# Two mixer projections from plain fp32 matmuls to three fp32r passes, with the remainders on VectorE in layer 0 and on GpSimd in layer 1

## The chip, the core and the metric

One core of a Trainium2 chip runs the whole program once. The metric is the device time of one execution in microseconds (us); the lower the better. The five engines of the core (TensorE, VectorE, ScalarE, GpSimd and SyncE, which issues the transfers) have queues of their own and meet at semaphores. The profile calls them PE, DVE, ACT, POOL and SP; PEld is TensorE's loading of stationary operands, which overlaps its matmuls.

## What is computed

A block of 256 tokens with 1024 features passes two layers of the first network (feed-forward, token mixer, feed-forward, a layer norm after each) and then two layers of a second one. All data is fp32. The part that the change touches is the first product of each token mixer:

```python
def token_mixer(h, w_in, pool_w, pool_scale, rel_bias, lb, norm_g, w_branch, w_out):
    proj = h @ w_in          # [256, 1024] @ [1024, 6920]
    (a, q, k, v, qi, ki, wi, hq, hf, hi, hg, gates) = jnp.split(proj, MIX_SPLITS, axis=-1)
    y_a = pool_mixer(a, pool_w, pool_scale)
    y_b = sparse_attention(q, k, v, qi, ki, wi, rel_bias)
    y_c = hgrn2(hq, hf, hi, hg, lb, norm_g)
    g = jax.nn.sigmoid(gates)
    return (g[0] * (y_a @ w_branch[:256]) + g[1] * (y_b @ w_branch[256:512])
            + g[2] * (y_c @ w_branch[512:])) @ w_out
...
    h = modulate(layer_norm(x), mod, 1)
```

## The kernel before

**Panels.** Every weight matrix is cut into panels of 256 output columns, 1 MB each, and streamed in the order of use through four SBUF slots by SP (`load`, L529). A panel's load waits until TensorE has finished the panel four places earlier. A product of the kernel is a `Gemm` in `plan()`; `Gemm(f"mix{l}", 15)` are the first 3848 columns of `w_in` in 15 panels, `gate{l}` the gates in 12.

**Two ways to multiply.** A plain panel (`features`, L674) multiplies the fp32 weights with the fp32 activations H; the profile shows each such matmul as two MATMUL rows of 256 columns, 32 a panel. A split panel (`split_up`, L703 to L705 for a stage's first panel, and `split_half`, L687 to L689 for the rest) has the fp32r rounding of the weights (high) and of the activations, and both remainders (low), and sums three products, high x high, high x low and low x high: 48 MATMUL rows of 256 columns. ScalarE makes a half panel's high part by a copy (`high`, L1379), another engine then its low part by a subtraction in place (`low`): VectorE for all the feed-forward products of the first network (L86), GpSimd for `even` and `up0` in the second (L1340). High parts lie in a ring of two panels, so ScalarE writes one only when TensorE has used the panel two places before (`wait_used`). TensorE waits for each half's `low_made`.

**The mixer's first stage.** Panels 0 to 4 and 9 to 14 hold features on the partitions, 6 to 8 are computed with tokens on the partitions (`tokens`, L765), and 5 is a mixed one: half a panel of features (L1232) and 16 narrow matmuls (L1235). ScalarE takes each result out of PSUM (`evac`, L76). All four accumulators of `acc` are in use in turn.

**Riders.** While TensorE works on these panels, VectorE computes something else: the modulation vectors, from 1 MB panels of their own ("cond units": `cond_weigh`, L1959; 15 of them in each mixer). A cond unit is a multiply with row sums of [128, 1024] by a row of conditions that is spread over the partitions: two such instructions in layer 0, four in layer 1 (there two condition rows are served). The units alternate between two SBUF slots, and SP loads unit i only when `cond_done` says that unit i - 2 is finished. SP runs one list in order: panel u, unit u, panel u + 1, unit u + 1, and so on. So a panel's load also stands behind the wait of the unit before it:

```python
load(g, it * 4 + u, u)         # after TensorE has finished panel u - 4
load_cond(g.name, it, u)       # waits cond_done of unit u - 2
```

**Around it.** `layer_norm` runs before each stage on four engines; for j = 0 (the one ahead of a mixer) it writes H alone, the even chunks by ScalarE and the odd ones by VectorE, and TensorE starts chunk by chunk. For j = 1 and 2 (ahead of split panels) it also makes high and low parts of the activations (L1414, L1416, and L86 for the subtraction). After the 15 panels `stage_end` joins TensorE, VectorE and ScalarE: none goes on until all three have come. Then come `pool`, `attention` and `hgrn`, with the gate panels between.

## Time and profile before

| | us |
|---|---|
| median of 3 runs | 3105.27 (3104.22 to 3106.03) |
| profiled execution, its time | 3109.24 |
| its span | 3107.4 |
| TensorE busy | 2791.2 (90%) |
| VectorE busy | 1874.8 (60%) |
| ScalarE busy | 1034.5 (33%) |
| GpSimd busy | 197.8 (6%) |
| last mean matmul of the layer norm ahead of mixer 0, of mixer 1 | 256.98, 986.97 |
| stage of mixer 0, first matmul to the join | 267.25 to 373.26 |
| stage of mixer 1, first matmul to the join | 997.29 to 1103.30 |

The two stages are 106.0 us each, 7% of the span together. Busy shares are averages over stages of different kinds; what a stage gains by the change has to be read in that stage.

### The profile page before, as it was taken

Reading aid. Unit: us, or ns where it says so; the run is one execution under the profiler, and the core shown is the slowest. Engines: PE = TensorE matmul, PEld = TensorE weight load, DVE = VectorE, ACT = ScalarE, POOL = GpSimd, SP = SyncE. Lnnn points to the kernel's source line nnn. Section 1 sums busy time; section 2 is a strip of 40 time slices with the busy share of each in tenths; the row PEclk is TensorE's granted clock in tenths of the full one; section 3 lists DMA queues with packets and bytes.
Section 4 is the critical chain, followed back from the end, with each engine's and each line's share of the span. In section 5 each row is a group of like instructions: output and inputs, shape, how many; then the busy total and the mean of one; then the engine's idle time right before and its main releaser. Section 6 shows DMA issues by size and latency. Waiting matters only on the chain.

```text
span 3107.4 us, 47661 instructions
## 1 busy us (share of the span) xinstructions
PE 2791.2 (90%) x18018; PEld 2348.9 (76%) x18018; DVE 1874.8 (60%) x3213; ACT 1034.5 (33%) x1334; POOL 197.8 (6%) x89
## 2 busy tenths in 40 slices
PE   2999999999999998999799467999999799969998
PEld 2998877999998887899688344587745567648887
DVE  5785254677785844657482675577733576662881
ACT  1432132443542123243433542333301544441211
POOL 0000000000000000000044000144300000000000
PEclk9999999999999998999899579999999999979999
DMA  7786633577673932456151101122252211103441
GB/s 267 269 320 253 231 109 141 203 263 281 222 274 129 342 123 84 175 188 240 66 211 55 63 1 63 67 95 94 83 219 111 82 68 68 55 14 122 150 173 70
DMA packets 109673, 469.59 MB, mean 151 GB/s; under 512 B 7020, under 2 KB 60856, under 8 KB 62136
## 3 DMA queue, kind: packets, MB, share of 16 engines
q1 hardware_dynamic: 109496, 467.19, 41.6%
q8 instruction: 116, 1.90, 0.2%
q14 instruction: 61, 0.50, 0.0%
HBM read 466.10 MB, written 1.06 MB: 150 GB/s over the span
## 4 chain that ended last, share of the span: by engine, by line
issue 52%; PE 30%; DVE 8%; DVEq 6%; ACT 3%; ACTq 1%; POOLq 0%; PEldq 0%; PEld 0%
PE accs L786 9%; DVEq L2570 3%; PE accs L674 3%; DVE arena L2547 2%; PE accs L687 2%; PE accs L689 2%; PE accs L688 2%; PE accs L1134 2%; PE accs L1135 2%; PE accs L1136 2%; DVE normed L86 1%; ACT arena L76 1%; PE mix L1182 1%; DVE arena L86 1%; PE mix L833 1%
## 5 line engine op out<-in xcount | busy, mean ns | idle before, releaser
L687 PE MATMUL accs<-normed_r,arena_r 128*128 128x256 f32 (+2 forms) x1864 | 585.6, 314 | 20.4 <-DVE cond_panel_r L86 6.1
L688 PE MATMUL accs<-arena_r 128*128 128x256 f32 (+1 forms) x2090 | 594.8, 285 | 0.0
L689 PE MATMUL accs<-normed_r,panel_r 128*128 128x256 f32 (+2 forms) x1872 | 585.0, 312 | 0.0
L674 PE MATMUL accs<-normed,panel 128*128 128x256 f32 x2176 | 483.8, 383 | 6.7 <-ACTq L469 3.0
L674 PEld LDWEIGHTS accs<-normed,panel 128*128 128x128 f32 x2176 | 413.9, 192 | 71.3 <-issue 4.6
L86 DVE TENSOR_TENSOR panel_r<-panel,arena_r 128x1024 fp32r<-128x1024 f32 (+1 forms) x240 | 319.7, 1332 | 130.5 <-ACTq L1380 91.2
L688 PEld LDWEIGHTS accs<-arena_r 128*128 128x128 f32 x2090 | 395.5, 189 | 2.2 <-issue 0.2
L687 PEld LDWEIGHTS accs<-normed_r,arena_r 128*128 128x128 f32 (+1 forms) x1864 | 351.2, 188 | 56.4 <-issue 13.0
L1379 ACT ACTIVATE arena_r<-panel 128x1024 fp32r<-128x1024 f32 (+1 forms) x240 | 275.3, 1147 | 303.4 <-PE accs L689 114.6
L689 PEld LDWEIGHTS accs<-normed_r,panel_r 128*128 128x128 f32 (+1 forms) x1872 | 350.8, 187 | 23.9
L2547 DVE SCALAR_TENSOR_TENSOR arena<-accs,vectors,arena 128x189 f32<-128x189 f32 (+2 forms) x704 | 279.3, 428 | 95.2 <-issue 66.0
L1340 POOL TENSOR_TENSOR panel_r<-panel,arena_r 128x1024 fp32r<-128x1024 f32 x74 | 183.6, 2481 | 2046.6 <-ACTq L1387 2045.0
L786 PE MATMUL accs<-arena,panel 128*128 128x256 f32 (+1 forms) x960 | 284.8, 458 | 0.6 <-DVEq L2568 0.6
L786 PEld LDWEIGHTS accs<-arena,panel 128*128 128x128 f32 x960 | 183.1, 191 | 100.8 <-issue 84.7
L76 ACT ACTIVATE arena<-accs 128x512 f32<-128x512 f32 (+2 forms) x128 | 75.3, 588 | 458.4 <-PE accs L674 198.6
L91 DVE SCALAR_TENSOR_TENSOR residual<-accs,mods,residual 128x256 f32<-128x256 f32 x96 | 46.4, 484 | 291.9 <-PE accs L786 177.4
L687 PE MATMUL accs<-arena_r 128*128 128x256 f32 x704 | 202.5, 288 | 6.4 <-DVEq L2000 6.4
L689 PE MATMUL accs<-arena_r,panel_r 128*128 128x256 f32 x704 | 200.1, 284 | 0.0
L76 ACT ACTIVATE arena<-residual 128x512 f32<-128x512 f32 (+1 forms) x64 | 36.9, 577 | 370.4 <-DVEq L2599 300.4
L1386 ACT ACTIVATE arena_r<-panel 128x1024 fp32r<-128x1024 f32 x74 | 78.5, 1061 | 229.8 <-PE accs L689 200.9
L76 ACT ACTIVATE arena<-arena 128x512 f32<-128x512 f32 (+7 forms) x107 | 97.3, 909 | 161.3 <-DVEq L2493 54.6
L687 PEld LDWEIGHTS accs<-arena_r 128*128 128x128 f32 x704 | 135.3, 192 | 7.5 <-issue 6.9
(373 smaller groups left out, 4151.8 us busy)
## 6 DMA issues: line engine op xcount, KB each, us to landing
panel<-w SPq DMA_DIRECT2D x250, 1024.0 KB, 4.9
panel<-w SPq DMA_DIRECT2D x48, 1408.0 KB, 7.8
cond_panel<-wc SPq DMA_DIRECT2D x56, 1024.0 KB, 7.0
normed<-wc SPq DMA_DIRECT2D x48, 1024.0 KB, 7.5
arena<-wc SPq DMA_DIRECT2D x16, 1024.0 KB, 5.7
residual<-xs SPq DMA_DIRECT2D x2, 1024.0 KB, 8.3
residual<-crows SPq DMA_DIRECT2D x2, 512.0 KB, 8.8
arena<-cond_row_kept SPq DMA_DIRECT2D x2, 512.0 KB, 6.8
```

The costliest lines, as they stand in the source:

```text
L76: i = self.eng.activation(*a, **k)
L86: i = self.eng.tensor_tensor(*a, **k)
L674: mm = pe.matmul(acc[b][:, o:o + ntok], w[:, k * PANEL + j * P:k * PANEL + j * P + P], rhs(k), start=(k == 0), stop=(k == KD - 1))
L687: pe.matmul(out, hi[:, k, 0:m], src_hi(k), start=clear and k == 0, stop=False, skip_group_check=True)
L688: pe.matmul(out, hi[:, k, 0:m], src_lo(k), start=False, stop=False, skip_group_check=True)
L689: mm = pe.matmul(out, lo[:, k, 0:m], src_hi(k), start=False, stop=last and k == n - 1, skip_group_check=True)
L786: mm = pe.matmul(acc[a % BANKS][:, o:o + ntok], w[:, k * PANEL + j * P:k * PANEL + j * P + P], src(part * kper + k), start=first, stop=(pa ...
L1340: pool.tensor_tensor(lo, half_panel(g, u, j), hi, ALU.subtract)
L1379: act.eng.activation(split_parts(g, u, j)[0], half_panel(g, u, j), ACT.Copy)
L1386: act.eng.activation(split_parts(g, u, j)[0], half_panel(g, u, j), ACT.Copy)
L2547: dve.eng.scalar_tensor_tensor(out=out, in0=src, scalar=scale, in1=out, op0=ALU.mult, op1=ALU.add)
L2570: dve.drain()
```

## The change

Both `mix` products become split ones. In each mixer TensorE now does 48 MATMUL rows of 256 columns in the place of 32 for the feature panels and for the three token panels (`mix_tokens`), and for panel 5 24 in the place of 16, with the 32 narrow rows as they were (`mix_keys`). ScalarE makes the high parts (`mix_high`, a ring of two panels in the room of the gates), two halves a panel and one for panel 5: 29 copies a mixer. The 29 subtractions are VectorE's in mixer 0 (`mix_low`, ahead of each cond unit) and GpSimd's in mixer 1 (`POOL_LOW`). The layer norm ahead of a mixer now makes high and low parts of the activations as well; the fp32 values stay in H for the gates and for panel 5. Loads, cond units, gates and all that follows stay as they were.

```diff
@@ plan
-                  Gemm(f"mix{l}", 15), Gemm(f"gate{l}", 12), ...
+                  Gemm(f"mix{l}", 15, split=True, kept=True), Gemm(f"gate{l}", 12), ...
+POOL_LOW = ('mix1',)
+        mix_hi = [region(7472 + i * KD * PANEL, KD, PANEL, of=arena_r) for i in range(2)]
+        m_hi, m_lo = region(15664, KD, T, of=arena_r), region(17712, KD, T, of=arena_r)
+        def mix_halves(u):
+            return ((0, 2),) if u == 5 else ((0, 1), (1, 1))
+        def norm_target(l, j):
+            if j == 2:
+                return G[f"in{l + 1}0"] if l + 1 < DEPTH else None
+            if j == 1:
+                return G[f"in{l}1"]
+            return G[f"mix{l}"] if G[f"mix{l}"].split else None
@@ tensor
+            def mix_keys(g, u):
+                b = acc_open(g, 0, u)
+                w = slots[(g.p0 + u) % SLOTS]
+                split_half(g, 0, u, 0, acc[b][:, 0:T], lambda k: m_hi[:, k, :], lambda k: m_lo[:, k, :], True, True, first_used)
+                for tb in range(2):
+                    for k in range(KD):
+                        mm = pe.matmul(acc[b][:, T + 8 * tb:T + 8 * tb + 8], H[:, k, T + tb * P:T + tb * P + P],
+                                       w[:, k * PANEL + P:k * PANEL + P + 8], start=False, stop=(k == KD - 1), skip_group_check=True)
+                mm.then_inc(ready[b], 1)
+            def mix_tokens(g, u):
+                hi, lo = mix_hi[u % 2], slots_r[(g.p0 + u) % SLOTS]
+                b = acc_open(g, 0, u)
+                pe.wait_ge(S("low_made"), split_count(g, 0, u, 1))
+                for tb in range(2):
+                    t = slice(tb * P, tb * P + P)
+                    for k in range(KD):
+                        pe.matmul(acc[b][:, tb * T:tb * T + T], m_hi[:, k, t], hi[:, k, :], ...)
+                        mm = pe.matmul(acc[b][:, tb * T:tb * T + T], m_lo[:, k, t], hi[:, k, :], ...)
+                mm.then_inc(first_used, 1)
+                for tb in range(2):
+                    for k in range(KD):
+                        mm = pe.matmul(acc[b][:, tb * T:tb * T + T], m_hi[:, k, tb * P:tb * P + P], lo[:, k * PANEL:k * PANEL + PANEL], ...)
+                mm.then_inc(ready[b], 1)
@@ gpsimd, ahead of all else
+            for name in POOL_LOW:
+                g = G[name]
+                for u in range(g.n):
+                    for j, count in mix_halves(u):
+                        pool.wait_ge(S("high_made"), split_count(g, 0, u, count - 1 if u == 5 else j))
+                        pool.tensor_tensor(half_panel(g, u, j, slots_r), half_panel(g, u, j), split_parts(g, u, j)[0], ALU.subtract)
+                        pool.drain().then_inc(S("low_made"), count)
@@ scalar
+            def mix_high(g, u):
+                s = (g.p0 + u) % SLOTS
+                act.wait_ge(landed[s], 16 * ((g.p0 + u) // SLOTS + 1))
+                for j, count in mix_halves(u):
+                    wait_used(act, g, 0, u - 2, j)
+                    act.eng.activation(split_parts(g, u, j)[0], half_panel(g, u, j), ACT.Copy)
+                    act.drain().then_inc(S("high_made"), count)
@@ scalar layer_norm
-                if j == 1:
+                if j < 2:
                     wait_ready(act, g, 0, 3)
...
-                            act.eng.activation(h_hi[:, k, :], X[:, k, lat], ACT.Identity, scale=scale, bias=bias)
+                            act.eng.activation((m_hi if j == 0 else h_hi)[:, k, :], X[:, k, lat], ACT.Identity, scale=scale, bias=bias)
@@ scalar, mixer stage
                         for u in range(15):
+                            if g.split and 2 <= u < 14:
+                                mix_high(g, u + 1)
                             if u == 0:
                                 evac(g, 0, u, 0, apad[:, :, PAD:PAD + T], both, ACT.Copy)
@@ vector layer_norm
-                if j == 1:
+                if j < 2 and mine:
                     low(after, 0, 0)
...
-                if after is not None:
+                if mine:
                     low(after, 0, 1)
@@ vector, mixer stage
                         for i in range(CARRY[f"mix{l}"][1]):
+                            if G[f"mix{l}"].split and f"mix{l}" not in POOL_LOW and 2 <= i + 1 < 15:
+                                mix_low(G[f"mix{l}"], i + 1)
                             cond_weigh(f"mix{l}", i, i % 2)
```

The order of VectorE's instructions at the start of mixer 0, before. L111 to L81 are the end of the layer norm (X is `residual`, H is `normed`), the L1959 rows are cond units of two instructions each, whose panels lie in `normed` and `cond_panel` in turn.

```order
L86 TENSOR_TENSOR residual<-residual,std 128x2x256
L81 TENSOR_SCALAR normed<-residual,ln_vectors 128x256
L1959 SCALAR_TENSOR_TENSOR normed,mods<-normed,constants 128x4x256 [waits cond_landed0]
L1959 SCALAR_TENSOR_TENSOR normed,mods<-normed,constants 128x4x256
L1959 SCALAR_TENSOR_TENSOR cond_panel,mods<-cond_panel,constants 128x1024 [waits cond_landed1]
L1959 SCALAR_TENSOR_TENSOR cond_panel,mods<-cond_panel,constants 128x1024
```

And with the change (the same helper now has line L2036).

```order
L86 TENSOR_TENSOR residual<-residual,std 128x2x256
L81 TENSOR_SCALAR normed<-residual,ln_vectors 128x256
L86 TENSOR_TENSOR arena_r<-normed,arena_r 128x512 [waits h_parts] x2
L86 TENSOR_TENSOR panel_r<-panel,arena_r 128x8x128 [waits high_made] x2
L2036 SCALAR_TENSOR_TENSOR normed,mods<-normed,constants 128x4x256 [waits cond_landed0]
L2036 SCALAR_TENSOR_TENSOR normed,mods<-normed,constants 128x4x256
L86 TENSOR_TENSOR panel_r<-panel,arena_r 128x8x128 [waits high_made] x2
L2036 SCALAR_TENSOR_TENSOR cond_panel,mods<-cond_panel,constants 128x1024 [waits cond_landed1]
L2036 SCALAR_TENSOR_TENSOR cond_panel,mods<-cond_panel,constants 128x1024
L86 TENSOR_TENSOR panel_r<-panel,arena_r 128x8x128 [waits high_made] x2
```

The cond units of mixer 0 now stand behind the subtractions of panels 1 to 14, and each subtraction pair behind the unit before it.

In mixer 1 VectorE's cond units stay next to each other, four instructions each. The subtractions are in GpSimd's list, of which this is the start before (`even`'s first panel):

```order
L1340 TENSOR_TENSOR panel_r<-panel,arena_r 128x8x128 [waits high_made] x2
```

and with the change:

```order
L1406 TENSOR_TENSOR panel_r<-panel,arena_r 128x8x128 [waits high_made] x29
L1398 TENSOR_TENSOR panel_r<-panel,arena_r 128x8x128 [waits high_made] x2
```

The 29 of mixer 1 (panels 0 to 14, one for panel 5) come ahead of those that GpSimd had already; each waits for its high part alone, and not for anything of VectorE's.

## Rows read from the trace of the kernel before

**Rows 1.** The page, part 1: busy time, share of the span, instructions.

```profile
PE 2791.2 (90%) x18018; PEld 2348.9 (76%) x18018; DVE 1874.8 (60%) x3213; ACT 1034.5 (33%) x1334; POOL 197.8 (6%) x89
```

**Rows 2.** Timeline (start us, us, engine, line, operation [idle before]): mixer 0, both joins.

```profile
289.53 0.60 ACT L76 ACTIVATE arena<-accs 128x512 f32<-128x512 f32 x1 [6.31 <-PE accs L674]
...
373.26 14.08 PE L674 MATMUL accs<-normed,panel 128*128 128x256 f32 x64 [0.77 <-ACTq L469]
...
1103.30 8.90 PE L674 MATMUL accs<-normed,panel 128*128 128x256 f32 x40 [0.77 <-ACTq L469]
```

**Rows 3.** Timeline, ScalarE in a split feed-forward stage: a result every two panels.

```profile
1349.35 0.60 ACT L76 ACTIVATE arena<-accs 128x512 f32 x1 [4.71 <-PE accs L689]
1360.64 0.60 ACT L76 ACTIVATE arena<-accs 128x512 f32 x1 [4.69 <-PE accs L689]
```

**Rows 4.** Timeline, TensorE at two layer norms: the last mean matmul, the first panel.

```profile
256.98 1.13 PE L802 MATMUL mix<-residual,ones_d 128*128 128x256 f32 x4 [0.27 <-DVE residual L91]
267.25 1.10 PE L674 MATMUL accs<-normed,panel 128*128 128x256 f32 x4 [0.72 <-ACT normed L76]
...
564.40 1.13 PE L802 MATMUL mix<-residual,ones_d 128*128 128x256 f32 x4 [0.27 <-DVE residual L91]
576.91 0.36 PE L703 MATMUL accs<-normed_r,arena_r 128*128 128x256 f32 x1 [1.17 <-DVE arena_r L86]
```

**Rows 5.** Timeline, a split feed-forward stage: ScalarE high parts, VectorE subtractions.

```profile
563.30 2.21 ACT L1379 ACTIVATE arena_r<-panel 128x1024 fp32r<-128x1024 f32 x2 [29.48 <-PE accs L674]
...
585.03 1.23 DVE L86 TENSOR_TENSOR panel_r<-panel,arena_r 128x1024 fp32r<-128x1024 f32 x1 [0.21 <-ACTq L1380]
586.43 1.23 DVE L86 TENSOR_TENSOR panel_r<-panel,arena_r 128x1024 fp32r<-128x1024 f32 x1 [0.17 <-issue]
```

**Rows 6.** SP's timeline, mixer 1; transfers: panels in mixer 0, units in mixer 1 (us to landing).

```profile
1016.58 0.57 SPq L557 DMA_DIRECT2D normed<-wc  x1
1017.35 0.51 SPq L529 DMA_DIRECT2D panel<-w  x1
...
panel<-w SPq DMA_DIRECT2D x13, 1024.0 KB, 5.2
...
normed<-wc SPq DMA_DIRECT2D x7, 1024.0 KB, 6.6
```

**Rows 7.** Timeline, VectorE in mixer 1: two units' starts, what follows the last.

```profile
1001.00 1.23 DVE L1959 SCALAR_TENSOR_TENSOR constants<-normed,residual 128x1024 f32<-128x1024 f32 x1
...
1005.95 1.23 DVE L1959 SCALAR_TENSOR_TENSOR constants<-cond_panel,residual 128x1024 f32<-128x1024 f32 x1
...
1087.81 0.46 DVE L86 TENSOR_TENSOR mods<-mods,vectors 128x30 f32<-128x30 f32 x2
```

**Rows 8.** Timeline in the stage `even`: VectorE, then GpSimd beside it.

```profile
1590.13 1.23 DVE L1959 SCALAR_TENSOR_TENSOR arena<-arena 128x1024 f32<-128x1024 f32 x1 [0.27 <-DMA arena<-wc]
1591.28 3.43 DVE L1959 SCALAR_TENSOR_TENSOR arena<-arena 128x1024 f32<-128x1024 f32 x1
1594.79 3.25 DVE L1959 SCALAR_TENSOR_TENSOR arena<-arena 128x1024 f32<-128x1024 f32 x1
...
1608.62 1.23 DVE L1959 SCALAR_TENSOR_TENSOR arena<-arena 128x1024 f32<-128x1024 f32 x1
...
1590.26 3.36 POOL L1340 TENSOR_TENSOR panel_r<-panel,arena_r 128x1024 fp32r<-128x1024 f32 x1 [6.45 <-ACTq L1387]
1593.86 3.10 POOL L1340 TENSOR_TENSOR panel_r<-panel,arena_r 128x1024 fp32r<-128x1024 f32 x1 [0.24 <-issue]
```

**Rows 9.** Instructions of a line, all of the span: minimum/median/maximum in ns.

```profile
L1340 POOL TENSOR_TENSOR panel_r<-panel,arena_r x74: 2344/2408/3356, 1529.9 to 2228.3; 128x1024 fp32r<-128x1024 f32 x74
...
L86 DVE TENSOR_TENSOR normed<-residual,std x40: 424/692/2680, 1532.1 to 3100.8; 128x512 f32<-128x512 f32 x24, 128x256 f32<-128x256 f32 x16
...
L2547 DVE SCALAR_TENSOR_TENSOR arena<-accs,vectors,arena x704: 401/415/482, 1998.9 to 3035.3; 128x189 f32<-128x189 f32 x88, 128x252 f32<-128x252 f32 x44, 128x192 f32<-128x192 f32 x44
```

**Rows 10.** Busy time in a stretch: PE, PEld, DVE, ACT, POOL, granted clock, DMA share, GB/s.

```profile
1540.00:1560.00 20.00, 13.79 (x34) 7.96 (x33) 6.68 (x10) 15.97 (x25) 4.72 (x2) 0.68 0.40 144
```

More of the change, by code:

```diff
@@ L496, in split_parts, with h_index @@
             return hi, half_panel(g, u, j, slots_r)
+        def h_index(l, mixer, f=0):
+            return 2 * l + f + (1 if mixer else 0) + sum(1 for m in range(l + f) if G[f"mix{m}"].split)
+        def mix_halves(u):
+            return ((0, 2),) if u == 5 else ((0, 1), (1, 1))
         def split_count(g, it, u, j):
             return it * 8 + (2 * (g.s0 + u) + j + 1)
+        def norm_target(l, j):
[4 more added lines that the diff above has]
+            return G[f"mix{l}"] if G[f"mix{l}"].split else None
         def wait_used(eng, g, it, u, j):
@@ L1389, in layer_norm @@
             def layer_norm(n, l, j, g):
-                after = None if j == 0 or (j == 2 and l + 1 == DEPTH) else G[f"in{l}1" if j == 1 else f"in{l + 1}0"]
+                after = norm_target(l, j)
                 act.activation(rms_cols[:, 16:17], eps_ln, ACT.Sqrt)
-                if j == 1:
+                if j < 2:
                     wait_ready(act, g, 0, 3)
@@ L1420, in layer_norm @@
                     else:
-                        act.wait_ge(S("h_odd"), (l + 1) * KD // 2)
+                        act.wait_ge(S("h_odd"), (1 if G["mix0"].split else l + 1) * KD // 2)
                     for k in range(KD):
@@ L2000, in low, with mix_low @@
                     dve.drain().then_inc(S("low_made"), 1)
+            def mix_low(g, u):
+                for j, count in mix_halves(u):
+                    dve.wait_ge(S("high_made"), split_count(g, 0, u, count - 1 if u == 5 else j))
+                    dve.tensor_tensor(half_panel(g, u, j, slots_r), half_panel(g, u, j), split_parts(g, u, j)[0], ALU.subtract)
+                    dve.drain().then_inc(S("low_made"), count)
             def residual(g, l, gate0, norms_done):
@@ L2040, in layer_norm @@
                 dve.wait_ge(S("mean_ready"), n + 1)
-                after = None if j == 0 or (j == 2 and l + 1 == DEPTH) else G[f"in{l}1" if j == 1 else f"in{l + 1}0"]
+                after = norm_target(l, j)
+                mine = after is not None and after.name not in POOL_LOW
                 for k in range(0, KD, 2):
                     dve.tensor_tensor(X[:, k:k + 2, lat], X[:, k:k + 2, lat], bc(mix[:, 0, 0:T], 2), ALU.subtract).then_inc(S("centred"), 2)
-                if j == 1:
+                if j < 2 and mine:
                     low(after, 0, 0)
```

41 lines of the change are left out of this document (28 added, 13 removed).

## The prediction

> **What bounds the kernel now.** I read four views. The page's first part shows TensorE busy for 90% of the span [rows 1], so removed TensorE time can count; but a share is a mean over stages, so the two stages of the change have to be read in the timeline. There a result of mixer 0 leaves every 6.91 us, an idle time of 6.31 and a copy of 0.60, released by TensorE [rows 2]: TensorE sets the pace, and each stage ends in a join, at 373.26 and 1103.30. SP's and VectorE's timelines then show what else runs in a chain in these stages, the cond units. Last I looked for a place where GpSimd subtracts while VectorE works on two SBUF operands; there is one, in the stage `even`.
>
> **TensorE's part.** A split feed-forward stage gives a result every two panels, 1349.35 to 1360.64 [rows 3]: 5.65 us a panel, so 1.26 less than 6.91. Panel 5 keeps its narrow half; it loses about half of that, 0.6. If TensorE stayed the bound, 14 panels behind the first would give 13 x 1.26 + 0.6 = 17 us a mixer, 34 in all.
>
> **The layer norm ahead.** Today the first matmul comes 10.3 us after the last mean matmul; ahead of a split stage it is 12.5 [rows 4]. So the first panel starts 2.2 later and is itself 1.26 shorter: +1.0 us at its end, in each mixer.
>
> **Mixer 0: a chain takes over.** SP issues panel u + 2 behind unit u + 1, which waits for unit u - 1; and on VectorE unit u - 1 now stands behind the subtractions of panel u. The round that serves two panels is: a unit of two instructions 2.5 (half of 4.95, [rows 7]); SP's issue of the next unit, then the panel, 0.8; the panel's landing 5.2 [rows 6]; the first half's copy 1.1 and both subtractions at 1.4 each [rows 5]. That is 12.4 for two panels, 6.2 a panel, above TensorE's 5.65. VectorE alone would need 2 x 1.4 + 2.5 = 5.3 and is not the bound; ScalarE has 2.2 + 0.6. Panels 1 and 2 are loaded in time and run at 5.65, the other 12 at 6.2: 85.7 against 14 x 6.91 = 96.7, a gain of 11.0. Off it go 1.0 of the norm, about 1 because unit 0 (and with it the load of panel 3) starts later, and about 1 at the end, where VectorE has two units left after the last subtraction. **Mixer 0: -8 us.** Bounds: TensorE's own pace all the way gives 17 - 1 = -16; if the landings stretch to 6.6 as the units' do [rows 6] the round is 13.8, 6.9 a panel, and nothing is left: 0. I take the middle because 5.2 is a median measured in this very stage.
>
> **Mixer 1: two engines, one port.** Here VectorE has four unit instructions a panel, and GpSimd two subtractions. What they do to each other can be read in `even` [rows 8]. VectorE's instruction of 1591.28 took 3.43 us instead of 1.23: GpSimd's had begun at 1590.26, itself had waited for VectorE's first, and ended at 1593.62; VectorE's ended 1.1 later. The next pair does the same. From 1590.13 to 1608.62 VectorE did eight such instructions while GpSimd did four. Alone eight take 2 x 4.95 = 9.9; they took 18.5. So a subtraction by GpSimd costs VectorE (18.5 - 9.9) / 4 = 2.15 us, nearly all of its own 2.41 [rows 9]. This is a turn-taking, not a slowdown: work that both have to do adds up. The Trainium skill (SBUF — State Buffer, "Who interferes with whom") says that a VectorE instruction with two SBUF inputs and a GpSimd one that reads SBUF block each other for a whole instruction. By that rule the price would be the full 2.41, and the sum below 6 us higher. An instruction of VectorE with one operand in PSUM was never held up, at most 482 ns over 704 of them [rows 9]; the units have none in PSUM.
>
> The stage's sum: today the units run from 1001.00 to 1087.81 [rows 7], 86.8 us, of which 15 x 4.95 = 74.3 is work and 12.5 waits for loads (a load takes 6.6, and there are two slots). With the change they start later by the norm: 2.2, about 1.5 (an estimate) for the four subtractions of activations that VectorE now ends with, and 3.7 because GpSimd subtracts panel 1 exactly while VectorE normalises: two blocks of 2.15, less what falls into gaps. That such normalisations are held up, 2680 instead of 692 ns, stands among the instructions by line [rows 9]. Start: 1008.4. Behind it lie 25 of the 29 subtractions (panels 2 to 14, one for panel 5): 25 x 2.15 = 53.7. A unit with its share of blocks lasts 4.95 + 2 x 2.15 = 9.2, longer than a load, so the 12.5 of waiting vanishes. End: 1008.4 + 74.3 + 53.7 = 1136.4, then 0.6 of vector sums and the join at about 1137.3 instead of 1103.3: **+34 us.** TensorE doesn't come later: panel 14 is issued when unit 11 is done, and its landing (5.2), copy (1.1), blocked subtractions (2 x 3.4) and product (5.65) take 19 us, while units 12 to 14 take 23. What is queued behind the units on SP is the panels, each behind a unit's `cond_done`; so TensorE gets one panel in 9.2 us and idles 3.5 of them. Its clock may fall in those gaps; in the stretch of 1540 to 1560, with TensorE busy for 13.8 of 20 us, the granted clock was 0.68 of full [rows 10], so part of it at the lower level of 1.2 GHz. A panel at 1.2 GHz would be 11.3 instead of 5.65; in single panels the slack hides that. After the join I add 1 us for matmuls at the lower clock.
> Bounds of the stage: if GpSimd cost VectorE nothing, the units would start at 1004.7 and keep today's 86.8, to 1091.5, and TensorE, whose last panel needs 5.65 behind its subtractions, would end about 1096: -7. If each subtraction costs the full 2.41 and the 12.5 of load waits stay, it is 34 + 6.5 + 12.5 = +53.
>
> **The sum.** -8 + 34 + 1 = +27 us. The profiled execution took 3109.24; that makes 3136. It lies 4.0 above the median of the runs, so against 3105.27 I predict 3132 and, since the rule and a later start of the units both lie above, 3133. No cover is lost elsewhere: the gate panels behind panel 14 are issued before the join, as they are now.
>
> **The rivals.**
> Rival A, faster: GpSimd's subtractions run beside the units at no price. The point that decides is whether a unit instruction of VectorE goes on for 1.23 us when GpSimd starts. Against it stands `even` [rows 8]; for it only that the operands lie elsewhere in SBUF (units in `normed` and `cond_panel` instead of `arena`). Then mixer 1 gives -7, mixer 0 -8: 3105.3 - 15 = 3090. Both mixers at TensorE's pace would be 3105 - 32 = 3073, the lowest end.
> Rival B, half the blocks: half of GpSimd's port time falls into VectorE's drains and waits for loads, so the stage pays 27 us and not 54. For it speaks that today 12.5 us of waits are there to be filled; against it that a unit which takes 9.2 never waits for a load of 6.6. Then mixer 1 gives +34 - 27 = +7: 3105.3 + 7 - 8 + 1 = 3105; with anything between half and full, 3105 to 3120.
> Rival C, slower still: the clock. TensorE's bursts of 2.8 us with idle times between could keep it at 1.2 GHz for most of the stage; a panel is then 11.3 us, more than 9.2. From the first matmul, 997.3 + 2.2 + 3.7 = 1003, panel 0 with 8 and 14 more with 158 give 1169: +66, in all 3105.3 + 66 - 8 = 3163. The stretch from 1540 on shows that the lower level comes only in part [rows 10]; and a TensorE that has become the bound is busy without gaps, and in the split feed-forward stages a panel never takes more than about 5.65. The Trainium skill (TensorE: Matmul & The Clock Gate, "HAM oscillation — how this bites in real kernels") tells of kernels where waits in every round bring the lower level back each time; that would be this rival's case.
> Rival D, a pace by GpSimd: two subtractions that wait for VectorE's instruction each time, 2 x (2.4 + 1.1) = 7.0 a panel, under 9.2, so it can't set the pace alone; no chance of its own.
>
> **How the numbers follow.** Forecast, blocks nearly in full: 0.70. A: 0.12. B: 0.12. C: 0.06. A measurement of this kernel tells 0.2%, 6 us, from no change. Faster by more: A and nearly none of B, 0.13. Within 6 us: the low end of B, 0.05. Slower: 0.82. The range goes from the middle of B's stretch, 3113, to the forecast with the full price, half of the load waits and no gain left in mixer 0, 3133 + 6 + 6 + 8 = 3153, which I cut to 3150: it leaves out A, half of B and C.
>
> **What would show it.** VectorE's unit instructions (today all 1.22) with about 25 to 30 of them at 3.2 to 3.5 us in mixer 1, and none in mixer 0; GpSimd busy 29 times, 2.4 to 3.4 us each; the stage of mixer 1 (last mean matmul to join, 116.3 us today) at 150, that of mixer 0 (116.3 too) at 108; SP waiting for VectorE before nearly every unit; TensorE idle 3 to 4 us a panel in mixer 1, released by GpSimd, and half a microsecond in mixer 0, released by VectorE. The prediction is wrong if unit instructions keep 1.23 beside GpSimd's, or if TensorE has no idle time in mixer 1.

## The result, and the profile after

The changed kernel took 3152.66 us (median of 6 runs, 3152.02 to 3155.6). The kernel before, run beside it, took 3110.01 (6 runs, 3104.22 to 3120.31; the three shown ahead of the prediction are among them). The ratio is 1.0132, with an interval of 1.0115 to 1.0149: 41 us slower. I had predicted 3133, with a range up to 3150. The sign of the whole and the mechanism of mixer 1 held. In mixer 0, where I had forecast a gain, the change loses.

The profiled execution took 3152.02 us against 3109.24 before. The page's first part answers to [rows 1]:

```profile
PE 2778.1 (88%) x18482; PEld 2358.6 (75%) x18482; DVE 1975.8 (63%) x3250; ACT 1103.9 (35%) x1408; POOL 283.6 (9%) x118
```

TensorE is busy for 13 us less and the kernel is 43 us longer; VectorE is busy for 101 us more. The timeline gives the landmarks: both last mean matmuls, ScalarE's last result and VectorE's first copy at the join of mixer 0, TensorE at the join of mixer 1 [rows 2, 4].

```profile
258.67 1.13 PE L853 MATMUL mix<-residual,ones_d 128*128 128x256 f32 x4 [0.27 <-DVE residual L91]
...
380.27 0.60 ACT L76 ACTIVATE arena<-accs 128x512 f32<-128x512 f32 x1 [5.05 <-PE accs L712]
...
380.99 0.17 DVE L96 COPY arena<-arena 128x2 f32<-128x2 f32 x1 [1.05 <-ACTq L474]
...
992.40 1.13 PE L853 MATMUL mix<-residual,ones_d 128*128 128x256 f32 x4 [0.27 <-DVE residual L91]
...
1146.62 3.58 PE L697 MATMUL accs<-normed,panel 128*128 128x256 f32 x8 [6.20 <-DVEq L474]
```

Mixer 0 takes 122.3 us from its mean matmul to VectorE's first copy at the join (116.3 before), mixer 1 takes 154.2 (116.3), counted from the modulation sum at 992.44. Before, TensorE's last result ended both stages, and VectorE stood idle for 17.05 and 14.82 us at the joins. Now TensorE's last panel, with ScalarE's copy of it, still ends mixer 0, but VectorE waits only 1.05 us there; mixer 1 is ended by VectorE, and TensorE waits 6.20 for it. At that join the kernel is 43.3 late (1146.62 against 1103.30), and at the end 42.8: 6.0 and 37.9 arise in the two mixers, and -1.1 in all the rest.

VectorE and GpSimd at the start of mixer 1's blocks, in the timeline, answer to [rows 7, 8]:

```profile
1022.90 1.22 DVE L2036 SCALAR_TENSOR_TENSOR normed<-normed,residual 128x1024 f32<-128x1024 f32 x1
...
1024.25 3.23 DVE L2036 SCALAR_TENSOR_TENSOR constants<-cond_panel,residual 128x1024 f32<-128x1024 f32 x1
...
1027.41 3.42 DVE L2036 SCALAR_TENSOR_TENSOR cond_panel<-cond_panel,residual 128x1024 f32<-128x1024 f32 x1
...
1030.91 1.23 DVE L2036 SCALAR_TENSOR_TENSOR constants<-cond_panel,residual 128x1024 f32<-128x1024 f32 x1
...
1023.55 2.84 POOL L1406 TENSOR_TENSOR panel_r<-panel,arena_r 128x1024 fp32r<-128x1024 f32 x1 [11.97 <-ACTq L1454]
1026.57 3.18 POOL L1406 TENSOR_TENSOR panel_r<-panel,arena_r 128x1024 fp32r<-128x1024 f32 x1 [0.18 <-issue]
```

GpSimd's instruction (1023.55) starts inside VectorE's of 1022.90 and waits for its end, and the next one of VectorE (1024.25) waits for GpSimd's end at 1026.39. So it goes on: two of VectorE's take 3.23 and 3.42 us instead of 1.23, and the third is quick again. Of the 60 unit instructions in mixer 1, 25 took over 2 us; in mixer 0, where GpSimd is idle, none of 30 did. The units ran from 1019.30 to 1145.84, 126.5 us, with 74.3 of work: (126.5 - 74.3) / 25 = 2.09 us for each subtraction behind their start.

The waits in mixer 0 (engine, line, who was waited for: us in total, times, longest), and the transfers there (KB each, median us to landing), which answer to [rows 6]:

```profile
ACT arena_r L1443 <- DMA panel<-w: 39.9, 12, 5.7
DVE panel_r L86 <- ACTq L1444: 28.5, 11, 5.5
PE accs L710 <- DVEq L2084: 12.2, 6, 3.2
```

```profile
panel<-w SPq DMA_DIRECT2D x16, 1024.0 KB, 7.8
normed<-wc SPq DMA_DIRECT2D x7, 1024.0 KB, 5.8
```

Read upwards from TensorE: it waits for VectorE's subtraction, VectorE for ScalarE's high half, ScalarE for the panel. A panel lands 7.8 us after its issue, not 5.2. SP's own waits say why it is issued so late, and SP's timeline how:

```profile
SPq L580 <- DVEq L2037: 105.0, 13, 31.6
SPq L552 <- PE accs L712: 6.0, 2, 5.3
```

```profile
281.62 0.55 SPq L580 DMA_DIRECT2D normed<-wc  x1
282.22 0.65 SPq L552 DMA_DIRECT2D panel<-w  x1
286.92 0.33 SPq L580 DMA_DIRECT2D cond_panel<-wc  x1
288.06 0.34 SPq L552 DMA_DIRECT2D panel<-w  x1
296.31 0.61 SPq L580 DMA_DIRECT2D normed<-wc  x1
297.11 0.50 SPq L552 DMA_DIRECT2D panel<-w  x1
```

Each panel goes out some 0.6 us behind a 1 MB unit. From 281.62 to 296.31 two panels go out: 14.7 us, 7.3 a panel, more than the 6.91 of the plain stage. The six rounds up to 370.94 took 13.7 to 16.3 us, 14.9 in the mean. SP's waits and timeline in the kernel before, and its transfers in mixer 0, show what has changed places:

```profile
SPq L529 <- PE accs L674: 31.0, 8, 6.6
...
303.50 0.34 SPq L529 DMA_DIRECT2D panel<-w  x1
304.10 0.56 SPq L557 DMA_DIRECT2D normed<-wc  x1
```

```profile
normed<-wc SPq DMA_DIRECT2D x7, 1024.0 KB, 7.5
cond_panel<-wc SPq DMA_DIRECT2D x6, 1024.0 KB, 7.6
```

There SP waited for TensorE to free a panel's slot, issued the panel, and the unit right behind it: panels landed in 5.2 [rows 6], units in 7.5. Now SP waits for `cond_done`, issues the unit, and the panel right behind it: units land in 5.8, panels in 7.8. In both, the second of the pair is the late one, and the change of the wait made the panel the second.

The kernel before shows the same thing within its mixer 1, whose loads I had read in [rows 6] for the units alone. Up to 1045 SP issued each unit ahead of a panel, from 1060 on each panel ahead of a unit. The transfers of the first stretch (1005 to 1045), then of the second (1060 to 1085):

```profile
panel<-w SPq DMA_DIRECT2D x7, 1024.0 KB, 8.0
normed<-wc SPq DMA_DIRECT2D x4, 1024.0 KB, 6.2
...
panel<-w SPq DMA_DIRECT2D x4, 1024.0 KB, 5.0
normed<-wc SPq DMA_DIRECT2D x2, 1024.0 KB, 8.1
```

So the later landing of a panel behind a unit could be read before the change was made. No run turned the pair around in the split stage with all else kept; that its order makes the landing late is read from these stretches.

TensorE's granted clock in mixer 0 was 0.92 of full (1.00 before), which is 10 us of its time. TensorE was idle for 16.9 of the 122.3 us, so the chain hides part of that; how much of the last one or two microseconds is the clock's is open.

### The profile page after: what moved, and what is told of

The parts are those of the page before. It is cut to its first block, busy times and chain, and to the rows that moved or that the text cites. A ratio compares the mean times of both kernels' runs of the same rounds, so it can differ in the third digit from the quotient of the medians.

```text
span 3150.2 us, 48912 instructions
## 1 busy us (share of the span) xinstructions
PE 2778.1 (88%) x18482; PEld 2358.6 (75%) x18482; DVE 1975.8 (63%) x3250; ACT 1103.9 (35%) x1408; POOL 283.6 (9%) x118
## 4 chain that ended last, share of the span: by engine, by line
issue 51%; PE 28%; DVE 8%; DVEq 6%; POOLq 4%; ACT 2%; ACTq 1%; PEldq 0%; PEld 0%
PE accs L837 9%; DVEq L2656 3%; POOLq L1407 3%; PE accs L697 2%; DVE arena L2633 2%; PE accs L1185 2%; PE accs L710 2%; PE accs L712 2%; PE accs L711 2%; PE accs L1186 2%; PE accs L1187 2%; POOLq L1399 1%; DVE normed L86 1%; ACT arena L76 1%; PE mix L1233 1%
## 5 line engine op out<-in xcount | busy, mean ns | idle before, releaser
L711 PE MATMUL accs<-arena_r 128*128 128x256 f32 (+1 forms) x2426 | 693.0, 286 | 0.0
L711 PEld LDWEIGHTS accs<-arena_r 128*128 128x128 f32 x2426 | 463.2, 191 | 2.1 <-issue 0.2
L86 DVE TENSOR_TENSOR panel_r<-panel,arena_r 128x1024 fp32r<-128x1024 f32 (+1 forms) x269 | 355.3, 1321 | 160.8 <-ACTq L1454 91.0
L1453 ACT ACTIVATE arena_r<-panel 128x1024 fp32r<-128x1024 f32 (+1 forms) x252 | 288.0, 1143 | 340.4 <-PE accs L712 141.7
L697 PE MATMUL accs<-normed,panel 128*128 128x256 f32 x1472 | 331.4, 386 | 9.8 <-DVEq L474 6.2
L710 PE MATMUL accs<-arena_r 128*128 128x256 f32 x1040 | 303.1, 291 | 40.4 <-POOLq L1407 20.9
L697 PEld LDWEIGHTS accs<-normed,panel 128*128 128x128 f32 x1472 | 282.3, 193 | 54.1 <-DVEq L474 6.4
L712 PE MATMUL accs<-arena_r,panel_r 128*128 128x256 f32 x1040 | 298.3, 287 | 0.0
L1398 POOL TENSOR_TENSOR panel_r<-panel,arena_r 128x1024 fp32r<-128x1024 f32 x74 | 184.5, 2494 | 951.9 <-ACTq L1461 950.3
L710 PEld LDWEIGHTS accs<-arena_r 128*128 128x128 f32 x1040 | 203.1, 195 | 45.0 <-issue 42.6
L712 PEld LDWEIGHTS accs<-arena_r,panel_r 128*128 128x128 f32 x1040 | 203.1, 195 | 0.0
L1406 POOL TENSOR_TENSOR panel_r<-panel,arena_r 128x1024 fp32r<-128x1024 f32 x29 | 84.8, 2926 | 1051.9 <-ACTq L1454 1013.1
```

The lines of the kernel that those rows point to most:

```text
L86: i = self.eng.tensor_tensor(*a, **k)
L697: mm = pe.matmul(acc[b][:, o:o + ntok], w[:, k * PANEL + j * P:k * PANEL + j * P + P], rhs(k), start=(k == 0), stop=(k == KD - 1))
L710: pe.matmul(out, hi[:, k, 0:m], src_hi(k), start=clear and k == 0, stop=False, skip_group_check=True)
L711: pe.matmul(out, hi[:, k, 0:m], src_lo(k), start=False, stop=False, skip_group_check=True)
L712: mm = pe.matmul(out, lo[:, k, 0:m], src_hi(k), start=False, stop=last and k == n - 1, skip_group_check=True)
L1398: pool.tensor_tensor(lo, half_panel(g, u, j), hi, ALU.subtract)
```

## The experiments

Theory 1: in mixer 1 GpSimd and VectorE take turns. Theory 2: in mixer 0 the panel loads, issued behind the units, set the pace. Rivals: the bandwidth of the mixed loads; TensorE's clock; some effect of one mixer on the other. Each run has one profiled execution, from which the stage times come.

All stage times in one table. "Mixer 0" is from the last mean matmul to VectorE's first copy at the join, "mixer 1" from the modulation sum at the end of its preceding stage to the same copy; both are 116.3 us before. "Behind" is the rest of the span. Ratios are to the kernel before, run beside each; its median was 3112.74 us beside runs 1 to 4, 3113.20 beside 5 to 8 and 3110.64 beside 9 to 12.

| Run | median us | ratio (interval) | mixer 0 | mixer 1 | behind |
|---|---|---|---|---|---|
| before | 3110.01 | | 116.3 | 116.3 | 2004.1 |
| the change | 3152.66 | 1.0132 (1.0115 to 1.0149) | 122.3 | 154.2 | 2003.6 |
| 1 mixer 0 alone | 3113.91 | 1.0011 (0.9998 to 1.0025) | 120.6 | 116.7 | 2000.3 |
| 2 mixer 1 alone | 3154.06 | 1.0132 (1.0107 to 1.0156) | 119.6 | 154.4 | 2010.2 |
| 3 VectorE subtracts | 3145.14 | 1.0109 (1.0083 to 1.0136) | 119.3 | 144.1 | 2007.2 |
| 4 mixer 0, panels first | 3095.88 | 0.9945 (0.9926 to 0.9964) | 105.0 | 116.7 | 2003.0 |
| 5 as 3, panels first | 3111.84 | 1.0014 (0.999 to 1.0038) | 102.9 | 130.8 | 2003.4 |
| 6 the change, panels first | 3144.28 | 1.0108 (1.0088 to 1.0129) | 102.9 | 155.8 | 2012.6 |
| 7 no blocks in mixer 1 | 3112.89 (1 run) | | 120.8 | 115.9 | 2001.6 |
| 8 before, panels first | 3109.43 | 0.9992 (0.9977 to 1.0007) | 116.3 | 116.3 | 2004.5 |
| 9 VectorE takes two panels | 3153.67 | 1.0134 (1.0106 to 1.0162) | 122.9 | 148.9 | 2009.5 |
| 10 GpSimd in mixer 0 | 3119.88 | 1.0026 (1.0013 to 1.0038) | 123.2 | 118.0 | 2004.7 |
| 11 GpSimd copies | 3118.32 (1 run) | | 120.2 | 113.6 | 2007.3 |
| 12 eight of fifteen split | 3100.39 | 0.9962 (0.9949 to 0.9975) | 102.9 | 116.4 | 2004.2 |

### Runs 1 and 2: one mixer at a time

```diff
-Gemm(f"mix{l}", 15, split=True, kept=True)
+Gemm(f"mix{l}", 15, split=(l == 0), kept=True)   # run 1, with POOL_LOW = ()
+Gemm(f"mix{l}", 15, split=(l == 1), kept=True)   # run 2
```

> Mixer 0 as changed, mixer 1 as before (exact four-pass panels, no subtraction). If the loads' chain sets mixer 0 (each panel is issued behind a modulation block that waits for the block two before it, and lands 7.8 us later), the stage takes 122 us again from the last mean matmul to VectorE's first copy (116.3 before) and the kernel comes out 5 to 7 us above the kernel before; 37 of the change's 43 us are gone. The forecast's terms would have 8 us less than before. If the two mixers' costs were not additive (a clock that stays low after mixer 0, for instance), mixer 1 would show more than 1 us of difference.

> Mixer 0 as before, mixer 1 as changed, with GpSimd's subtractions. If the two mixers add up: 36 to 39 us above the kernel before, and mixer 1 the same in each part as in the change (modulation blocks of 3.2 to 3.4 us an instruction, a stream of 126 us, the norm 13 us later). If the clock or the loads of mixer 0 had a part in it, the stream would be some us shorter.

Run 1 came out 3 us above its kernel before by the ratio, where 5 to 7 were expected, and its interval includes no change at all; run 2 came out 41 us above, where 36 to 39 were expected. Mixer 1 is the same with or without mixer 0's change (154.4 and 154.2), so the two are additive and nearly all of the loss is mixer 1's. Mixer 0 has to be read with care: in run 2 it is unchanged code and took 119.6. The busy time by stretch of that run (PE, PEld, DVE, ACT, POOL, granted clock, DMA share, GB/s) shows the 3.3 us:

```profile
279.30:299.30 20.00, 20.00 (x94) 17.60 (x94) 8.73 (x15) 1.75 (x3) 0.00 (x0) 1.00 1.03 404
299.30:319.30 20.00, 20.00 (x95) 17.59 (x94) 7.92 (x14) 1.21 (x4) 0.00 (x0) 0.83 0.95 344
```

TensorE is busy throughout, and the granted clock falls to 0.83 of full in one stretch, a third of it at 1.2 GHz: 3.4 us of product lost. It happens in an unchanged stage, so a difference of 3 us in one profile is not the code's. Split mixer 0 took 122.3, 120.6, 119.3, 120.8, 122.9 and 120.2 in six profiles (the change, runs 1, 3, 7, 9, 11): 121 us in the mean, 3 to 7 above the undisturbed plain stage.

### Run 3: mixer 1's subtractions on VectorE

```diff
-POOL_LOW = ('mix1',)
+POOL_LOW = ()
```

> Both mixers changed, with mixer 1's subtractions on VectorE. Theory 1 (GpSimd's subtraction and VectorE's instructions take turns at some 2.1 us each): without it a panel costs VectorE 2.8 us of subtraction and 4.95 of modulation block, 7.75 instead of 9.2, the norm loses its 9 us of held-up instructions, and mixer 1 is 22 to 28 us shorter than in the change (3125 to 3130). Theory 2 on top of it (the loads' chain, which now has VectorE's subtraction of the next panel ahead of each block): per two panels 0.8 + 7.8 + 1.1 + 2.8 + 4.95 = 17.5 us, 8.7 per panel, so only 10 to 15 us shorter than the change (3137 to 3142). The rival without turn-taking (GpSimd's subtractions cost VectorE nothing, the blocks are held up by something else): as VectorE gets 2.8 us of work more per panel, slower than the change by up to 35 us.

Mixer 1 is 10.1 us shorter (144.1), at the low end of the 10 to 15 that theory 2 on top of theory 1 had said; the median fell by 7.5, less than that. It goes against the rival without turn-taking: VectorE got 2.8 us of work more per panel and the stage became shorter. VectorE in the timeline:

```profile
1022.49 0.08 DVE L2036 DVE_READ_ACCUMULATOR cond_panel<-cond_panel,residual 128x1 f32 x1
1025.62 1.22 DVE L86 TENSOR_TENSOR panel_r<-panel,arena_r 128x1024 fp32r<-128x1024 f32 x1 [3.06 <-ACTq L1444]
1027.02 1.23 DVE L86 TENSOR_TENSOR panel_r<-panel,arena_r 128x1024 fp32r<-128x1024 f32 x1 [0.17 <-issue]
1028.41 1.23 DVE L2036 SCALAR_TENSOR_TENSOR constants<-normed,residual 128x1024 f32<-128x1024 f32 x1 [0.17 <-issue]
```

No product over 1.23 us is left. In its place stands a wait of some 3 us for ScalarE, once in two panels: the chain of loads, now in mixer 1 too, since the next panel is subtracted ahead of each unit.

### Runs 4, 5 and 6: SyncE issues panels one step earlier

```diff
+elif g.name in ('mix0',):            # runs 5 and 6: ('mix0', 'mix1')
+    for i in range(g.n + 1):
+        if i < g.n:
+            load_static(g, i)
+        if i >= 1:
+            load_cond(g.name, 0, i - 1)
 elif g.n >= 12 and g.ppa == 1:
```

Run 4 is run 1 with this, run 5 is run 3, run 6 is the change itself. A panel still stands behind a unit's wait, but for one unit earlier: each is issued one round ahead of where it was.

> Mixer 0 split with its subtractions on VectorE, mixer 1 as before; in mixer 0 SyncE issues panel u+1 ahead of modulation block u, so that no panel stands behind the wait for block u-1's predecessor. If that chain set mixer 0's 7.3 us per panel: it falls to TensorE's 5.65 us or the loads' own rate (two 1 MB loads per panel, 5.4 to 5.8 us), the stage gets 10 to 16 us shorter than in the run with mixer 0 alone and the kernel 5 to 12 us faster than the kernel before. If the bandwidth of mixed loads set it (panels landing 7.8 us because two loads are always in flight), it stays at +5 to +7.

> Both mixers split, all subtractions on VectorE, and SyncE issues panel u+1 ahead of modulation block u in both mixers. In the run with mixer 1's subtractions on VectorE it waited 2.7 to 3.1 us for ScalarE's high half once in two panels. If the loads' chain is behind that wait, mixer 1 goes at VectorE's own 7.75 us per panel: some 12 us less there, 15 us less in mixer 0, 26 to 28 us below that run, 3117 to 3120. If those waits are ScalarE's own doing, mixer 1 stays as it is and only mixer 0's 15 us go: 3129 to 3131.

> The change itself (GpSimd's subtractions in mixer 1) with panels issued ahead of the blocks in both mixers. Theory (turn-taking of GpSimd and VectorE alone sets mixer 1): mixer 1 keeps its 126 us stream of blocks and its norm held up by 9 us, only mixer 0 gains its 15 us: 3136 to 3140. If the loads had a share in mixer 1's stream, it gets shorter by more than 5 us: 3131 or less.

**Run 4** has mixer 0 at 105.0 instead of 120.6, within the 10 to 16 us that were expected. The kernel is faster than the one before: 0.9945, 17 us, more than the expected 5 to 12. The two profiled executions differ by 11.3 us, which is what the stage gained; the rest of the 17 is what separates these two executions from their medians. Busy time by stretch, and transfers, in its mixer 0:

```profile
280.00:300.00 20.00, 20.00 (x172) 20.00 (x171) 17.58 (x24) 13.68 (x19) 0.00 (x0) 1.00 0.76 286
300.00:320.00 20.00, 20.00 (x148) 20.00 (x146) 13.00 (x18) 7.35 (x10) 0.00 (x0) 0.83 0.94 360
320.00:340.00 20.00, 20.00 (x173) 20.00 (x172) 17.18 (x21) 10.23 (x11) 0.00 (x0) 1.00 0.94 343
```

```profile
panel<-w SPq DMA_DIRECT2D x15, 1024.0 KB, 9.0
normed<-wc SPq DMA_DIRECT2D x7, 1024.0 KB, 7.3
```

TensorE is busy without a gap for these 60 us. The DMA share rises to 0.94, so bandwidth was not the bound at 121 us. Nor was the clock: at 0.95 over this stage it was hardly higher than in run 1 (0.94), and the stage is 15.6 us shorter. A panel now needs 9.0 us to land, longer than before, and hardly anybody waits for it. What counted was the lead, not the landing time. ScalarE's waits for panels fell from 39.9 us to this one:

```profile
ACT arena_r L1449 <- DMA panel<-w: 1.1, 1, 1.1
```

**Run 5** gives mixer 1 130.8 instead of 144.1, and in the whole 33 us less than run 3, where 26 to 28 were expected (mixer 0 gave 16 and mixer 1 13; the other 4 lie behind the join). Its VectorE has no wait for the high half left there and was busy for 119.9 of 130.7 us: at its own 7.75 us a panel it is slower than plain TensorE's 6.91, so even without turn-taking mixer 1 loses 14.5 us by the split.

**Run 6** keeps mixer 1 at 155.8, as with the loads behind: theory 1 alone sets that stage. Mixer 0 gained 19 us, but the median fell by 8 only, to 4 us above what was expected. 9 us of the difference lie behind the join (2012.6 against 2003.6), in code that is the same: TensorE was busy there for 1793 us instead of 1781, at a granted clock of 0.93 instead of 0.94. Why the clock was lower is open; all four executions of this kernel took 3141 to 3146.

### Run 7: no blocks' arithmetic in mixer 1

```diff
-cond_weigh(f"mix{l}", i, i % 2)
+dve.wait_ge(cond_landed[slot], ...)      # mixer 1 only
+dve.drain().then_inc(S("cond_done"), 1)
```

> The change without the modulation blocks' arithmetic in mixer 1: the 60 products are left out there and their sums set to zero, the loads stay. If VectorE and GpSimd taking turns set the pace, then without VectorE's part GpSimd subtracts at the 2.36 us that its quickest took, 4.7 us per panel, TensorE gets its 5.65 us per panel, and the join comes 46 to 50 us earlier than in the change. If GpSimd's subtraction is 3.1 us by itself (6.2 per panel) the join comes some 38 to 42 us earlier; if the loads bound the stage (7.4 us to land), 30 us or less. The norm shows whether its instructions are held up by GpSimd as before: they should be, by 2.1 us each where a subtraction runs.

GpSimd's instructions (min/median/max in ns) behind the norm, and the busy time from TensorE's first product to the join:

```profile
L1406 POOL TENSOR_TENSOR panel_r<-panel,arena_r x25: 2343/2402/2419, 1024.6 to 1101.9; 128x1024 fp32r<-128x1024 f32 x25
```

```profile
1015.08:1109.40 94.32, 92.08 (x728) 91.54 (x728) 5.95 (x11) 45.39 (x58) 59.96 (x25) 0.93 0.84 312
```

Alone GpSimd needs 2.40 us, in the change 3.10 at the median: 0.7 of each is waiting for VectorE. TensorE is busy for 92.1 of 94.3 us, so its idle time in the change's mixer 1 comes from the pair of engines and not from GpSimd. Mixer 1 took 115.9 us, 38 less than in the change. By the number alone that is the expectation's second case (GpSimd's subtraction 3.1 us by itself, 38 to 42), and not the first (46 to 50); the 2.40 us decide against the second. What is missing is the clock: 15 panels at 5.65 are 84.8 us, and TensorE took 92.08 at a granted clock of 0.93 (92.08 x 0.93 = 85.6), so the clock took 7 us. The norm's instructions were held up as before (2.31, 2.28 and 2.25 us).

### Run 8: control, the kernel before with panels first

The same edit of SyncE's order, on the kernel before.

> Control: the kernel before with SyncE's panels issued ahead of the blocks in both mixers. There TensorE is the bound of both mixers at 6.91 us per panel, so the order of the loads alone should give nothing: within 0.15% of the kernel before. If it is faster by 0.3% or more, the gain of the run with mixer 0 split and panels first was the order's and not the three passes'.

The ratio is 0.9992, and both mixers stay at 116.3: the order alone gives nothing where TensorE is the bound. The gain of run 4 belongs to the three passes, once the panels are there in time.

### Run 9: VectorE subtracts the first two panels of mixer 1

```diff
-for u in range(g.n):
+pool.wait_ge(S("low_made"), split_count(g, 0, 1, 1))
+for u in range(2, g.n):
...
-mine = after is not None and after.name not in POOL_LOW
+mine = after is not None
```

> The change with the first two panels of mixer 1 subtracted by VectorE (four subtractions of 1.4 us inside its norm), GpSimd from panel 2 on. In the change the norm's instructions were held up four times by some 2.1 us while GpSimd subtracted, and the blocks started 26.9 us after the modulation sum; in the run with all subtractions on VectorE they started 20.9 us after it. If the turn-taking is what lengthens the norm: blocks start 21 us after the sum, no norm instruction over its usual length, and 5 to 7 us less than the change: 3145 to 3148. If the norm was late for another reason, no difference or up to 6 us more.

The stage did what was expected: the units start at 1015.13, 20.9 us after the sum at 994.22 (26.9 in the change), and mixer 1 is 5.3 us shorter. The two norms' lines tell the change's case; the change first, then run 9 (whose kernel numbers the first line one higher):

```profile
995.09 2.31 DVE L2117 TENSOR_SCALAR ln_vectors<-vectors 128x8 f32<-128x8 f32 x1
...
1005.27 1.75 DVE L111 RECIPROCAL std<-std 128x256 f32<-128x256 f32 x1 [4.39 <-ACT std L76]
1007.10 2.28 DVE L86 TENSOR_TENSOR residual<-residual,std 128x512 f32<-128x512 f32 x1
1009.48 2.26 DVE L81 TENSOR_SCALAR normed<-residual,ln_vectors 128x256 f32<-128x256 f32 x1
```

```profile
995.24 0.17 DVE L2118 TENSOR_SCALAR ln_vectors<-vectors 128x8 f32<-128x8 f32 x1
...
1001.76 1.75 DVE L111 RECIPROCAL std<-std 128x256 f32<-128x256 f32 x1 [0.17 <-ACT std L76]
1003.59 0.69 DVE L86 TENSOR_TENSOR residual<-residual,std 128x512 f32<-128x512 f32 x1
1004.37 0.41 DVE L81 TENSOR_SCALAR normed<-residual,ln_vectors 128x256 f32<-128x256 f32 x1
```

But the median did not fall (3153.67 against 3152.66, where 3145 to 3148 were expected): the part behind the join took 5.9 us more in this profile. As the kernel's time this run decides nothing; as a reading of the stage it does.

### Run 10: GpSimd subtracts in mixer 0

Run 4 with `POOL_LOW = ('mix0',)`.

> Mixer 0 split with panels first as in the fast run, but its subtractions on GpSimd; mixer 1 as before. VectorE would have only 2.5 us of block per panel left. Turn-taking: each subtraction takes GpSimd 2.4 us alone and 3.2 us beside a block, so 5.2 to 6.8 us per panel with the issue gap of 0.18, against TensorE's 5.65, and the norm ahead is held up by 6 to 9 us as in mixer 1: mixer 0 takes 112 to 124 us instead of 105, the kernel 3103 to 3115. If GpSimd's work cost nothing to the others, mixer 0 keeps its 105 us or gains the 2.8 us of the norm: 3093 to 3097.

Mixer 0 takes 123.2 us instead of 105.0, and the median is 24 us above run 4's. Here 20 of the 30 unit instructions of mixer 0 took over 1.5 us, up to 3.43, and GpSimd's subtractions 3.17 in the median. So the turn-taking belongs to the pair of engines and not to mixer 1. The stage is at the slow end of what was expected (112 to 124), the kernel 5 us beyond it. VectorE's idle time in mixer 0 was no shelter.

### Run 11: GpSimd copies instead of subtracting

```diff
-pool.tensor_tensor(half_panel(g, u, j, slots_r), half_panel(g, u, j), split_parts(g, u, j)[0], ALU.subtract)
+pool.tensor_copy(half_panel(g, u, j, slots_r), half_panel(g, u, j))
```

> The change with GpSimd copying each half panel (one input) where it subtracted (two inputs); the low halves then hold the whole panel rounded, so the third pass multiplies other numbers, in the same time. If turns are taken only when both engines read two operands from SBUF, VectorE's products go at 1.23 us throughout and mixer 1 falls to TensorE's or ScalarE's pace, 35 us or more below the change, near 3110 to 3117. If any work of GpSimd on SBUF holds VectorE up, its products still take over 2 us about 25 times, by the length of the copy.

GpSimd's copy and a pair of VectorE's products beside one:

```profile
L1406 POOL CAST panel_r<-panel x29: 1043/1810/2062, 995.6 to 1101.7; 128x1024 fp32r<-128x1024 f32 x29
```

```profile
1020.43 1.85 DVE L2036 SCALAR_TENSOR_TENSOR constants<-cond_panel,residual 128x1024 f32<-128x1024 f32 x1
...
1022.21 2.05 DVE L2036 SCALAR_TENSOR_TENSOR cond_panel<-cond_panel,residual 128x1024 f32<-128x1024 f32 x1
```

Neither side was quite right. VectorE is held up by a copy of one input as well (25 of its 60 products took 1.69 to 2.05 us), so two inputs on GpSimd are no condition. But the price follows the length of GpSimd's instruction: 0.5 to 0.8 us beside a copy of 1.05, 2.0 to 2.2 beside a subtraction of 2.4. So few of the products reach the 2 us that the second side had named, and the stage fell by 41 us to 113.6, as the first had said.

### Run 12: split as many panels as the engines balance

Run 5, but panels 2, 3, 4, 9, 10, 12 and 14 of mixer 1 go whole in four passes, without copy or subtraction.

> Subtractions on VectorE and panels first in both mixers, but in mixer 1 only eight of fifteen panels are split; panels 2, 3, 4, 9, 10, 12, 14 go whole, in four passes. From the run with all fifteen split, mixer 1 took VectorE 130.8 us from the modulation sum to its first copy; each whole panel takes 2.8 us off VectorE (7 x 2.8 = 19.6, to 111.2) and puts 1.26 us on TensorE (about 103 + 7 x 1.26 = 112). If that balance holds, mixer 1 takes 112 to 114 us against 116.7 with all panels whole, and the kernel is 3 to 5 us below the run with mixer 0 alone and panels first (3095.9). If the order of split and whole panels makes either engine wait, 117 us or more and no gain.

Mixer 1 takes 116.4 us, no gain over the plain 116.7, where 112 to 114 were expected. VectorE's waits for ScalarE are gone and TensorE was busy for 107.5 of 116.4 us, at a granted clock of 0.97 where the plain stage has 1.00: 3 us of it are the clock's. Run 4 has the lowest median; the two, 3095.88 and 3100.39, come from different sets of runs, and the intervals of their ratios overlap.

## Why the prediction was wrong where it was, and right elsewhere

The forecast was +27 us, 26 of them up to the second join; the joins say +43.3. By its own steps:

- **TensorE's part** held. With loads in time (run 4) the stage is 11.3 us shorter, and in runs 5, 6 and 12 it is 13.4 shorter, against the ceiling of -16; the granted clock, 0.95 in run 4 and 0.97 to 0.98 in the others, is 2 to 5 us of the difference.
- **Mixer 0, forecast -8, measured +6** (+3 to +7 over six profiles). This is the step that failed: the term "the panel's landing 5.2". It was read in a stage where for most of the time the panel was the first of each pair; I moved SP's wait to the unit and did not ask what that does to the order of the pair. Behind the unit it lands in 7.8. The round came to 14.9 us instead of 12.4, 7.4 a panel instead of 6.2, and 6.91 was the line between gain and loss. I trusted the 5.2 because it is "a median measured in this very stage"; it holds for the panels that lead their pair. My upper bound used the 6.6 of the units, the loads that led the pair in mixer 1, and so stopped at 0. The chain itself (unit, SP, load, copy, subtraction, unit) was named correctly, and run 4, which gave it one round of lead, took it off the stage's path. With the landing at 7.8 the same sum gives 15.0 a round, 7.5 a panel: 12 x (7.5 - 6.91) = 7 us lost there, 2.5 gained on panels 1 and 2, 3 lost at the ends: +7 to +8, a little above what was measured.
- **Mixer 1's stream, forecast 128.0, measured 126.5.** The price of a block, 2.15 from four of them in `even`, was 2.09 over 25; the load waits vanished as said; TensorE idled for up to 5.2 us a time for GpSimd. The stream has the size that was forecast. The sign "TensorE idle 3 to 4 us a panel" did not come: it waited 14 times for GpSimd, 25 us in all, 1.8 a time, since at a granted clock of 0.87 its panels filled more of the time.
- **Mixer 1's norm, forecast +7.4, measured +12.9** (26.9 from sum to first unit, 14.0 before). VectorE's four subtractions of activations cost 3.6, as forecast (2.2 + 1.5 = 3.7). The term "3.7 because GpSimd subtracts panel 1" was half: GpSimd also subtracts panel 0, and does so on the modulation sums and `ln_vectors`, which held up the centring by 4.2. Behind it two blocks cost 3.4. The rest, 1.7, is the variance's matmuls, 5.41 us instead of 3.72: TensorE had idled 4.68 us ahead of them, and in the stretch from 1000 to 1020 the granted clock was 0.67. These two parts, the panel that I left out and the clock, are why the stage exceeds its +34 by 4 us.
- **Tail.** Units end at 1145.84, 9.4 later than forecast (5.4 because the mixer starts later, 5.5 in the norm, less 1.5 in the stream), and the join follows 0.8 after them, as said.
- **After the join, forecast +1, measured -0.5**: nothing, within its scatter.
- **The page's rule.** The Trainium skill (SBUF — State Buffer, "Who interferes with whom") names VectorE instructions with two SBUF inputs as those that GpSimd's reads block, and `tensor_scalar` besides, with one, when it runs in a mode that uses both ports. The trace agrees that both kinds are held up: the norm's TENSOR_SCALAR took 2.26 us instead of 0.41; in which mode it ran no view shows. By the rule's whole instruction the price would be 2.41. It was 2.09 in the stream, and the norm's held-up instructions lost 1.6 to 2.1 each.
- **The rivals.** A and B fell: the products do not keep their 1.23. C did not come true: TensorE's clock was 0.87 of full over mixer 1, TensorE was busy for 112 of 154.2 us, and VectorE, not TensorE, ended it.

The 17 us between the forecast's 26 and the 43.3 are 14 in mixer 0 and 4 in mixer 1, with 1.7 ahead of mixer 0 and -2.3 between the mixers, in code that is the same. Against the medians a base comes on top that was low: 3105.27 of three runs, where the three later sets of the same kernel had medians of 3110.64 to 3113.20.

## What to carry to other kernels

When a change makes the engine that sets the pace faster, ask on what the queue that feeds it will wait next, and which load then goes out first: of two loads issued together the second landed some 2 us later here, and the old landing time is not the new one. Work moved to an engine that takes turns with a busy one was not free here and not even cheap; before moving it, add the moved duration to both engines, and count what it meets in the stage ahead too. A version with both points heeded, three passes in mixer 0 alone with panels issued one round earlier, beats the kernel before by 0.55% (interval 0.36 to 0.74).

## What the runs showed of the hardware

- GpSimd held VectorE up for most of its own instruction: 2.0 to 2.2 us beside a subtraction of 2.40, 0.5 to 0.8 beside a copy of 1.05; and itself lasted 3.10 and 1.81 at the median instead. Products (SCALAR_TENSOR_TENSOR), TENSOR_TENSOR and TENSOR_SCALAR of VectorE were held up, even one of 8 columns (2.31 instead of 0.17). Not held up were the products with one operand in PSUM [rows 9], of which 182 ran beside a subtraction, at 0.48 us at most. The norm's RECIPROCAL (1005.27, 1.75 us) had begun before the subtraction of 1006.48, which took its usual 2.35; there neither waited.
- Of two 1 MB loads issued within some 0.6 us of each other the first landed in 5.2 (panels before) or 5.8 us (units after), the second in 7.5 or 7.8, whichever of the two kinds it was. Issued one round earlier both took longer (7.3 and 9.0), at a DMA share of 0.94.
- The granted clock fell for a stretch in unchanged code with TensorE busy without gaps, 0.83 over 20 us, and that fall cost 3.4 us. The part behind the last join, the same code in all 14 kernels, took 2000 to 2013 us; its two longest cases (runs 2 and 6) had a granted clock of 0.93 there, the kernel before and the change 0.94. That is why the kernels' times alone do not tell 5 us apart, and a stage does so only with its clock beside it.
